# Expert gather and scatter with unsplit fp32 operands in a two-layer decoder step

## What is computed

```python
def swiglu(x, wg, wu, wd):
    return (jax.nn.silu(x @ wg) * (x @ wu)) @ wd

def moe(x, router_w, wg, wu, wd):
    ...
    logits = (xt @ router_w).astype(jnp.float32)
    top_v, top_i = lax.top_k(logits, TOP_K)
    gates = jax.nn.softmax(top_v, axis=-1)
    combine = jnp.sum(jax.nn.one_hot(top_i, N_EXPERTS, dtype=jnp.float32) * gates[..., None], axis=1)
    out = jnp.zeros_like(xt)
    for e in range(N_EXPERTS):
        out = out + combine[:, e:e + 1].astype(x.dtype) * swiglu(xt, wg[e], wu[e], wd[e])
```

## Time and profile before

| | |
|---|---|
| median of 3 runs | 1105.46 us (1104.29 to 1106.87) |
| profiled execution | 1102.1 us |
| its span, first to last instruction | 1100.3 us |
| mean granted TensorE clock | 0.992 |
| TensorE / VectorE / ScalarE busy | 95% / 71% / 58% of the span |
| expert stage | from about 630 us to the end |

### The profile page before, as it was taken

The page is one execution under the profiler, slowest core; times in us unless marked ns, Lnnn a source line. Parts: engine busy times, 40 slices in busy tenths (PEclk is TensorE's granted clock), DMA queues, the critical chain, the costliest instruction groups (busy, mean ns, idle before and its releaser), DMA issues.

```text
span 1100.3 us, 19864 instructions
## 1 busy us (share of the span) xinstructions
PE 1050.5 (95%) x7693; PEld 995.5 (90%) x7693; DVE 783.3 (71%) x1104; ACT 642.4 (58%) x861; POOL 22.6 (2%) x42
## 2 busy tenths in 40 slices
PE   6999999899999999999998979999999999999994
PEld 6999987799999999998986969899999999999983
DVE  6698743676555566789724478898888889888973
ACT  6476534564434445485524367777677767776761
POOL 1001000000000000002000000000000000000000
PEclk9999999999999999999999989999999999999998
DMA  9544579945555555443589619998989898898951
GB/s 373 199 167 141 185 272 354 351 155 193 179 189 175 181 179 189 167 141 121 180 318 357 230 57 374 329 365 283 354 295 363 286 342 314 317 334 316 349 211 42
DMA packets 64083, 272.99 MB, mean 248 GB/s; under 512 B 7200, under 2 KB 7328, under 8 KB 63360
## 3 DMA queue, kind: packets, MB, share of 16 engines
q1 hardware_dynamic: 62352, 264.33, 66.6%
q0 software_dynamic: 1504, 7.39, 1.8%
q10 hardware_dynamic: 144, 0.11, 0.0%
HBM read 265.83 MB, written 5.98 MB: 247 GB/s over the span
## 4 chain that ended last, share of the span: by engine, by line
PE 76%; DVE 13%; ACT 5%; DMA 3%; issue 2%; SPq 1%; DVEq 0%; ACTq 0%
PE bank L649 11%; PE bank L652 11%; PE bank L654 11%; PE bank L653 11%; PE bank L650 11%; PE bank L651 11%; DVE wl L1505 3%; DMA ring<-dense 2%; ACT wh L1108 2%; PE bank L676 2%; DVE rstd L1499 1%; DVE sq L1516 1%; PE bank L959 1%; PE bank L960 1%; PE bank L787 1%
## 5 line engine op out<-in xcount | busy, mean ns | idle before, releaser
L1505 DVE TENSOR_TENSOR wl<-ring,wh 128x1024 fp32r<-128x1024 f32 x170 | 206.2, 1223 | 162.6 <-ACT wh L1108 161.8
L649 PE MATMUL bank<-xh,wh 128*128 128x264 f32 x928 | 268.8, 290 | 12.3 <-DVE wl L1505 9.5
L1108 ACT ACTIVATE wh<-ring 128x1024 fp32r<-128x1024 f32 x170 | 178.0, 1055 | 167.2 <-PE bank L651 133.1
L1805 DVE TENSOR_TENSOR wl<-ring,wh 128x1408 fp32r<-128x1408 f32 x144 | 232.4, 1622 | 49.9 <-ACT wh L1366 49.6
L650 PE MATMUL bank<-xl,wh 128*128 128x264 f32 x928 | 265.2, 286 | 0.0
L651 PE MATMUL bank<-xh,wl 128*128 128x264 f32 x928 | 264.4, 285 | 0.0
L1366 ACT ACTIVATE wh<-ring 128x1408 fp32r<-128x1408 f32 x141 | 194.7, 1381 | 49.0 <-PE bank L654 47.4
L649 PEld LDWEIGHTS bank<-xh,wh 128*128 128x128 f32 x928 | 176.3, 190 | 18.4 <-issue 14.4
L653 PE MATMUL bank<-wh,xl 128*128 128x352 f32 (+4 forms) x560 | 184.2, 329 | 0.0
L650 PEld LDWEIGHTS bank<-xl,wh 128*128 128x128 f32 x928 | 176.6, 190 | 0.1
L651 PEld LDWEIGHTS bank<-xh,wl 128*128 128x128 f32 x928 | 176.0, 190 | 0.0
(11 more groups left out here) (263 smaller groups left out, 1709.6 us busy)
## 6 DMA issues: line engine op xcount, KB each, us to landing
ring<-experts SPq DMA_DIRECT2D x192, 704.0 KB, 5.8
ring<-dense SPq DMA_DIRECT2D x234, 512.0 KB, 4.3
o_k<-kv POOLq DMA_DIRECT2D x2, 1024.0 KB, 4.4
o_v<-kv POOLq DMA_DIRECT2D x2, 1024.0 KB, 7.4
x<-xT SPq DMA_DIRECT2D x2, 528.0 KB, 5.0
o_y<-sq SPq DMA_DIRECT2D x4, 264.0 KB, 2.1
mem<-memT SPq DMA_DIRECT2D x1, 1024.0 KB, 15.5
gatew<-gate_w POOLq DMA_DIRECT2D x2, 512.0 KB, 8.6
```

The lines of the kernel that those rows point to most:

```text
L649: mm(out, s_hi, m_hi, start=start, stop=False)
L1108: A(parts(k)[0], raw(u), ACT.Copy).then_inc(hi_ready, 1)
L1505: V.tensor_tensor(w_lo, raw(u), w_hi.bitcast(F32), ALU.subtract)\
L1805: V.tensor_tensor(w_lo, eraw(jj % ESLOTS), w_hi.bitcast(F32), ALU.subtract)\
```

## The change

The parts `tokh`, `tokl` become one fp32 array `tok`, and `eoh`, `eol` one fp32 array `eo`. `scat` is fp32, and the gather's moving operand is `gsel` read as fp32. Each pair of matmuls of the gather and of the scatter becomes one matmul with fp32 operands. VectorE's low parts of tokens and of expert outputs go, and ScalarE's copies now free the banks. TensorE waits for the rounded identity at `turn_scatter` instead of ahead of the first gather.

```diff
-        eoh = reuse("expert_out_hi", 2 * D)
-        eol = reuse("expert_out_lo", 2 * D)
-        scat = reuse("scatter", 2 * T)
+        eo = take(2 * D)
+        scat = take(2 * T)
...
-        tokh, tokl = chunks(hh_t, 3, D), chunks(hl_t, 3, D)
+        tok = chunks(nc.alloc_sbuf_tensor_at("token_rows", [P, 3 * D], F32, offset=hh_base), 3, D)
...
-                            slots = gsel[:, t, :, :].rearrange("p b s -> p (b s)")
-                            mm(out, tokh[:, t, f0:f0 + P], slots, start=(t == 0), stop=False)
-                            i = mm(out, tokl[:, t, f0:f0 + P], slots, start=False, stop=(t == 2))
+                            slots = gsel[:, t, :, :].rearrange("p b s -> p (b s)").bitcast(F32)
+                            i = mm(out, tok[:, t, f0:f0 + P], slots, start=(t == 0), stop=(t == 2))
...
                 pe.wait_ge(gcol_lo_ready, p + 1)
+                pe.wait_ge(ident_ready, 1)
...
-                        mm(b[:, 0:T], eoh[:, f0:f0 + P], s, start=(side == 0), stop=False)
-                        i = mm(b[:, 0:T], eol[:, f0:f0 + P], s, start=False, stop=(side == 1))
+                        i = mm(b[:, 0:T], eo[:, f0:f0 + P], s, start=(side == 0), stop=(side == 1))
...
-            pe.wait_ge(ident_ready, 1)
             run_pass(main)
...
-                    A(tokh[0:rows, t, hp * 512:(hp + 1) * 512], bank(n)[0:rows, :], ACT.Copy, scale=token_rstd[0:rows, t:t + 1])\
-                        .then_inc(oh_ready, 1)
+                    read(A(tok[0:rows, t, hp * 512:(hp + 1) * 512], bank(n)[0:rows, :], ACT.Copy,
+                           scale=token_rstd[0:rows, t:t + 1]), n)
...
-                    A(eoh[:, f0:f0 + 512], bank(n)[:, :], ACT.Copy, scale=gate[:, side:side + 1]).then_inc(eoh_ready, 1)
+                    read(A(eo[:, f0:f0 + 512], bank(n)[:, :], ACT.Copy, scale=gate[:, side:side + 1]), n)
...
-            for hp in range(2):
-                token_low(0, hp)
...
-                for u in range(2):
-                    n, more = num(f"D{u}")
-                    dve.wait_ge(eoh_ready, 2 * v + u + 1)
-                    cols = slice(side * D + u * 512, side * D + (u + 1) * 512)
-                    read(V.scalar_tensor_tensor(out=eol[:, cols], in0=bank(n)[:, :], scalar=gate[:, side:side + 1],
-                                                in1=eoh[:, cols].bitcast(F32), op0=ALU.mult, op1=ALU.subtract), n)
-                    upto(27)
+                upto(27)
...
-            for t in (1, 2):
-                for hp in range(2):
-                    token_low(t, hp)
...
-            G.memset(tokh[:, 2, :].bitcast(F32), 0.0).then_inc(tail_zeroed, 1)
-            G.memset(tokl[:, 2, :].bitcast(F32), 0.0).then_inc(tail_zeroed, 1)
+            G.memset(tok[:, 2, :], 0.0).then_inc(tail_zeroed, 1)
```

More of the change, by code:

```diff
@@ L250, in trunk_kernel @@
         assert NBUF * UNIT <= 3 * EUNIT
+        hh_base = -(-nc.sbuf_base // 32) * 32
         hh_t = sb("hidden_hi", [P, 12 * T], F32R)
@@ L465, in trunk_kernel @@
         gate_ready = sem("slot_gates_ready")
-        eoh_ready = sem("expert_out_hi_ready")
         x_final = sem("x_final")
@@ L1344, in _ @@
             A(token_rms[0:TS, 2:3], logits_sums[0:TS, 2:3, 32], ACT.Sqrt, bias=eps[0:TS, 0:1], scale=1.0 / D).then_inc(rms_ready, 1)
-            act.wait_ge(tail_zeroed, 2)
+            act.wait_ge(tail_zeroed, 1)
             act.wait_ge(rstd_ready, 1)
@@ L1839, in _ @@
             V.tensor_tensor(ed, ed, token_rstd, ALU.mult).then_inc(lmax_ready, 1)
-            def token_low(t, hp):
-                rows = TOK[t][1]
-                n = tiles[("tk", l, t, hp)]
-                cols = slice(hp * 512, (hp + 1) * 512)
-                dve.wait_ge(oh_ready, KC * DEPTH + 2 * t + hp + 1)
-                read(V.scalar_tensor_tensor(out=tokl[0:rows, t, cols], in0=bank(n)[0:rows, :], scalar=token_rstd[0:rows, t:t + 1],
-                                            in1=tokh[0:rows, t, cols].bitcast(F32), op0=ALU.mult, op1=ALU.subtract), n)
-            for hp in range(2):
-                token_low(0, hp)
             n = tiles[("ps", l)]
```

## The result

The changed kernel takes 1132.11 us at the median (1129.9 to 1133.83), the kernel before 1106.16 beside it: 26.0 us more, a ratio of 1.0243 with a 95% interval of 1.0219 to 1.0267. The profiled execution took 1129.9 us with a span of 1128.1.

A forecast was written before the change was run, and what follows sets the result against it. TensorE was taken to bound the expert stage, so its added time counts: 14.0 + 12.9 - 1.3 - 0.8 = +24.8 us, bringing the profiled execution to 1126.9 and, 3.4 us higher, the median to 1130.3; range 1125 to 1136.

The forecast's parts named there:

- Terms 1 and 2: Three later gathers, 72 fp32 matmuls at +0.195 us: +14.0 us; four scatters, 64 at +0.201 us: +12.9 us.
- Term 3: First gather: starts 4.2 us earlier, held by the gather matrix, then takes 10.4 us at full clock; -1.3 us for the stage.
- with an idle time of 1.7 us I expect none: First gather: TensorE's clock was expected not to fall after so short an idle time; at half clock the stage would be +0.6.
- rival B: First gather runs partly at half clock because TensorE was thinly used from 634 us on: 1132.2 us, chance 0.08.
- Term 4: Ahead of the last scatter: VectorE's low half of the last expert's output goes, -0.8 us.
- Terms 5 and 6: Identity's wait moved to `turn_scatter` and one POOL memset less: 0; VectorE's combine and weight low half behind longer scatters: 0.
- Rivals A, C and D: A: four starts per fp32 matmul, 1137.0 us, 0.05; C: weights' stream bounds, 1103.4, 0.03; D: cheap 0/1 operands, 1098, 0.02.
- One smaller sign: In the profile after, VectorE's busy time was to fall by 16 us, with nobody ending earlier for it.

## Why the prediction was right

The median of 1132.1 us lies 1.8 above the forecast of 1130.3 and inside the range of 1125 to 1136; the difference of the medians, 26.0 us, stands against 24.8. The two large terms were right in mechanism and size; the third had the wrong sign, and its error of 2 us was small enough for the range.

**Terms 1 and 2** held to the hundredth. 24 fp32 matmuls in 10.36 us are 0.432 us each, the figure taken from attention; three gathers cost 14.0 us. Four scatters cost 3 x 3.24 + 3.2 = 12.9. The scatter of 7.1 us that was to be seen is 6.93 to the first record of the turning and 7.13 with the 0.2 us that show in the turning. Nearly all of the result is these two products of a count and a distance of starts, both read from other lines of the kernel before.

**Term 3**, the first gather, was mis-sized. The start came 4.05 us earlier relative to the router (4.2 forecast), held by the gather matrix, as said; the identity's wait alone gave 1.3 us of it, and the other 2.7 came when VectorE's low halves of the tokens went too. But the step "with an idle time of 1.7 us I expect none", no fall of the clock, failed: the clock fell 0.9 us after the gather had begun, behind 1.91 us of idle time, and the gather took 11.93 us instead of 10.4. The stage cost +0.65 where -1.3 was counted; the other value that the prediction gave, +0.6 with the clock at half, was the right one. This is rival B, which had a chance of 0.08; it happened in both profiles of the changed kernel (+1.6 in the second), and all three other kernels with an fp32 gather that started this early took 11.9 to 13.3 us for it too.

What the step had wrong is that it took the length of the idle time for what decides. In the second execution of the changed kernel the clock had fallen before the gather began (timeline, then windows of TensorE: us, busy (x records), clock, DMA share, GB/s):

```profile
637.79 0.81 PE L944 MATMUL bank<-kv,ones 128*128 128x8 f32 x6
640.51 2.05 PE L959 MATMUL bank<-xh,token_rows 128*128 128x256 f32 x4 [1.91 <-DVE xh L1853]
...
638.00:639.00 1.00, 0.61 (x6) 1.00 0.00 0
639.00:640.00 1.00, 0.00 (x0) 0.53 0.00 0
```

It fell at about 639.05 us, 0.4 us after the router's last matmul had ended, where the prediction read "2.9 us after the last matmul" off one execution. In all 14 profiled executions the clock falls at this place, 2.3 to 5.1 us after the ranks' first matmul started, whether TensorE then stood still for 6.0, 4.6 or 1.9 us. What they share is what TensorE did ahead of it, which the prediction named for rival B: thin work with small matmuls. Which of it brings the fall stays open. B's figure of 1132.2 us lies 0.1 from the median; so close a match is luck, since single executions of the changed kernel took from 1129.9 to 1133.8.

**Term 4** was 0.8, as forecast (1.61 and 0.82 us). **Terms 5 and 6** held: no new wait in any pair, and the kernel with VectorE's work put back shows that its relief is worth nothing there.

**The falls in the first and last expert** were in no term. They make 3.1 us of the 27.8 between the two profiled executions. In the 26.0 between the medians their part is smaller, and by the mean granted clocks, which are alike in the two kernels, an estimate puts it near nothing; the runs don't resolve it.

**Rivals A, C and D** fell with the distances of the starts: 0.432 us is neither 0.474 nor 0.216, and no middle pair absorbed anything (a pair grew by 7.9 us, 4.67 + 3.24). Four passes, as the prediction names them from the Trainium skill ("FP8 and Floating Point Precision", TensorE Precision Notes), give the right order; priced at today's starts they would have been 10% too dear, 0.474 us for the 0.432 measured.

One smaller sign was wrong: VectorE's busy time fell by 11.0 us, not by 16. The 16 low halves had 11.9 us and the token ones 4.2, but the combine's 32 records, which now stand apart behind TensorE, take 13.3 us where 11.8 stood, and neighbouring records overlap by about 0.1 us, so a record taken out lowers the busy time by less than its length. I didn't test that further.

## What to carry to other kernels

Price a matmul by the distance between starts of its kind in the trace, not by its line count or by the duration in the row: here one fp32 matmul stood for two reduced-precision ones and cost 1.8 times their sum. Before an engine is relieved, look at who waits for whom: of the 16 us of VectorE's work that went, the 12 us at the expert outputs were worth 0.8 us and the 4 us at the tokens let one gather start 2.7 us earlier, while moving one VectorE instruction ahead of another, at the two places where TensorE did wait, was worth about 5. And a wait of one or two microseconds on TensorE may cost more than itself, by a fall of the clock behind it.

## What the runs showed of the hardware

An fp32 matmul with 128 stationary columns leaves two records, 0.216 us apart at 256 moving columns and 0.222 at 264, each with its own weight load; one in reduced precision takes 0.1185 and 0.1213.

The clock fell to half behind waits of TensorE of 1.2 and 2.4 us, once behind one of 0.62 us, and such a fall lengthened the stretches of the table by 1.2 to 1.6 us; behind the same wait of 1.22 us in another execution of the same kernel it didn't fall. Thirteen executions of the kernel before on one chip show how the clock and the spread of an unchanged kernel go together: those with a mean granted clock of 0.991 or 0.992 took 1100.0 to 1104.0 us, those with 0.983 to 0.985 took 1106.4 to 1108.6, and the one with 0.989 took 1104.2. The part ahead of the ranks' first matmul, where TensorE has the same 4995 records in all 14 profiled executions, took 635.6 to 641.7 us: up to 637.8 in those with the clock at half for some 3 us of it, 637.3 to 640.3 with some 7 us, and from 640.6 with some 10 us. A difference of a few microseconds between two profiled executions is therefore to be looked for in the clock's windows first.
